# Neighbourhood attention with products by four heads; token sums between halves of units; channel transforms copied by VectorE

## The reference, cut to what matters

```
for l in range(2):                                   # first block
    h = rms_norm(x, g_mix[l]); proj = h @ w_in[l]
    y_a = mla_mixer(...); y_b = dilated_mixer(...)
    y_c = neighbourhood_mixer(...)                   # 8 heads of 64, softmax over a window, then @ v
    merged = sum(sigmoid(gate_i) * (y_i @ w_pi[l]))
    x = x + merged @ w_o[l]
    h = rms_norm(x, g_ffn[l])
    x = x + (silu(h @ w1[l]) * (h @ w3[l])) @ w2[l]
x = rms_norm(x, g_final)
for l in range(2):                                   # second block
    h = layer_norm(x) * (1 + scale) + shift
    q, k, v, ... = split(h @ w_in2[l])
    y_attn = attention(rope(rms(q)), rope(rms(k)), v) * silu(g_a)
    y_conv = cb * short_conv(cc * cu) * silu(g_c)
    y_four = real(fft2(fu)) @ f_mix * silu(g_f)
    x = layer_norm(ALPHA * x + (1 + gate) * (concat(y) @ w_out[l])) * g + b
```

## Time and profile before

| | us |
|---|---|
| median of 3 runs | 2564.07 (2562.38 to 2568.13) |
| the profiled execution: time | 2568.33 |
| its span in the profile | 2566.5 |
| TensorE busy, matmuls | 2493.5 (97%) |
| GpSimd busy | 1938.6 (76%) |
| VectorE, ScalarE busy | 1128.2 (44%), 669.2 (26%) |

### The profile page before, as it was taken

One profiled execution on the slowest core, in us unless ns is written; L12 is line 12 of the kernel. 1 busy time (PEld: TensorE's weight loads), 2 busy tenths in 40 slices (PEclk: granted clock), 3 DMA queues, 4 the chain that ended last, 5 costly groups with the idle time before them and its releaser, 6 DMA issues.

```text
span 2566.5 us, 38041 instructions
## 1 busy us (share of the span) xinstructions
PE 2493.5 (97%) x12990; PEld 2002.1 (78%) x12990; DVE 1128.2 (44%) x1592; ACT 669.2 (26%) x1320; POOL 1938.6 (76%) x1567
## 2 busy tenths in 40 slices
PE   7999999999999999999999999999999999999998
PEld 6776777777888887777787777888887877778776
DVE  6557453224312125557634224422225338550765
ACT  4445232112201013435314111210002215231351
POOL 7788656899989889878764889998988574448704
PEclk9999999999999999999999999999999999999998
DMA  4233321223333323333421223333333121112301
GB/s 146 88 107 116 132 66 62 90 92 92 98 98 98 93 92 96 95 94 120 145 82 36 88 90 98 98 98 91 97 98 95 60 88 58 42 35 90 99 1 66
DMA packets 67569, 226.62 MB, mean 88 GB/s; under 512 B 7552, under 2 KB 16256, under 8 KB 66944
## 3 DMA queue, kind: packets, MB, share of 16 engines
q1 hardware_dynamic: 66016, 221.32, 27.4%
q10 hardware_dynamic: 1440, 3.79, 0.4%
HBM read 222.99 MB, written 2.10 MB: 88 GB/s over the span
## 4 chain that ended last, share of the span: by engine, by line
POOL 36%; PE 32%; issue 20%; DVE 5%; DMA 4%; POOLq 2%; ACT 0%; SPq 0%; DVEq 0%; ACTq 0%
POOL whi L477 18%; POOL wlo L480 12%; PE ps L575 8%; PE ps L577 8%; PE ps L576 8%; POOL raw L496 3%; POOL ada_acc L498 3%; DMA raw<-w_gate 2%; DMA raw<-w_abc 1%; PE ps L718 1%; PE ps L685 1%; DVE q_parts L1930 1%; POOLq L479 1%; PE ps L629 1%; PE ps L1133 1%
## 5 line engine op out<-in xcount | busy, mean ns | idle before, releaser
L477 POOL TENSOR_TENSOR whi<-raw,one 128x512 fp32r<-128x512 f32 (+3 forms) x732 | 793.4, 1084 | 505.0 <-PE ps L577 413.5
L480 POOL TENSOR_TENSOR wlo<-raw,whi 128x512 fp32r<-128x512 f32 (+3 forms) x732 | 955.7, 1306 | 57.4
L575 PE MATMUL ps<-h,whi 128*128 128x512 f32 (+1 forms) x1952 | 778.2, 399 | 27.3 <-POOL wlo L480 17.2
L576 PE MATMUL ps<-h,whi 128*128 128x512 f32 (+1 forms) x1952 | 764.6, 392 | 0.0
L577 PE MATMUL ps<-h,wlo 128*128 128x512 f32 (+1 forms) x1952 | 764.4, 392 | 0.0
L575 PEld LDWEIGHTS ps<-h,whi 128*128 128x128 f32 (+1 forms) x1952 | 368.1, 189 | 122.4 <-POOL wlo L480 30.0
L577 PEld LDWEIGHTS ps<-h,wlo 128*128 128x128 f32 (+1 forms) x1952 | 367.8, 188 | 79.1
L576 PEld LDWEIGHTS ps<-h,whi 128*128 128x128 f32 (+1 forms) x1952 | 368.4, 189 | 77.3 <-issue 2.4
L575 PE MATMUL ps<-y,whi 128*128 128x512 f32 x640 | 251.1, 392 | 0.6 <-DVE y L1852 0.6
L576 PE MATMUL ps<-y,whi 128*128 128x512 f32 x640 | 249.2, 389 | 0.0
L577 PE MATMUL ps<-y,wlo 128*128 128x512 f32 x640 | 249.2, 389 | 0.0
(11 more groups left out here) (290 smaller groups left out, 3059.7 us busy)
## 6 DMA issues: line engine op xcount, KB each, us to landing
raw<-w SPq DMA_DIRECT2D x120, 512.0 KB, 3.5
raw<-w_abc SPq DMA_DIRECT2D x68, 512.0 KB, 3.5
raw<-w_ada SPq DMA_DIRECT2D x48, 512.0 KB, 3.5
raw<-w_gate SPq DMA_DIRECT2D x48, 512.0 KB, 3.6
raw<-w_in SPq DMA_DIRECT2D x44, 512.0 KB, 3.5
raw<-w_pac SPq DMA_DIRECT2D x16, 512.0 KB, 3.5
raw<-w_o SPq DMA_DIRECT2D x16, 512.0 KB, 3.5
raw<-w_out SPq DMA_DIRECT2D x16, 512.0 KB, 3.5
```

The costliest lines, as they stand in the source:

```text
L477: pool.tensor_tensor(whi[:, s, r], raw[:, s, r], one[:, 0:1].to_broadcast([P, cols // 2]), ALU.mult).then_inc(hi_made, 1)
L480: pool.tensor_tensor(wlo[:, s, r], raw[:, s, r], whi[:, s, r].bitcast(F32), ALU.subtract).then_inc(made, 1)
L575: nc.tensor.matmul(out, whi[:, s, w], moving[:, c, :], start=(c == 0), stop=False)
L576: nc.tensor.matmul(out, whi[:, s, w], rest[:, c, :], start=False, stop=False)
```

## The change

Seven edits:

1. Start of a layer: square sums at the half of unit 2, the spread of the factor at the half of unit 3, and the three latent sums at the halves of unit 4, unit 15 and the unit behind unit 16, instead of between units.
2. Neighbourhood attention with `group=4`, and four slots for turned tiles instead of three.
3. Feed-forward: the first two units write banks 2 and 3 and do not wait for a bank; square sums at the half of the second unit, spread at the half of the third. VectorE's first round of the loop is written out with those banks.
4. `residual_and_input`: the rests of chunks 6 and 7 come before the squares of chunks 6 and 7.
5. Second block: `two_units` writes banks 2 and 3.
6. Channel transforms copied by VectorE, after its first three maxima, instead of by ScalarE.
7. `put_y` of the convolution's two tiles moves from before the attention into its steps 4 and 8; the attention's output gets a tile of its own (`out_g`) instead of `ytmp`.

```
-        slots_c = [pt_flat[:, i * C_WIN:(i + 1) * C_WIN] for i in range(3)]
+        slots_c = [pt_flat[:, i * C_WIN:(i + 1) * C_WIN] for i in range(4)]
...
-            def unit(s, n, moving, rest, m=P, each=None, halfway=None):
-
-                pe.wait_ge(bank_free[s], free_n[s].next())
+            def unit(s, n, moving, rest, m=P, each=None, halfway=None, bank=None):
+
+                if bank is None:
+                    pe.wait_ge(bank_free[s], free_n[s].next())
                 split_n[s].next()
-                tiles(s, s, n, moving, rest, m, each=each, halfway=halfway).then_inc(unit_done[s], 1)
+                tiles(s if bank is None else bank, s, n, moving, rest, m, each=each, halfway=halfway).then_inc(unit_done[s], 1)
...
                 unit(0, DC, h_hi, h_lo, each=chunk_by_chunk(h_ready, h_n, DC))
-                unit(1, DC, h_hi, h_lo)
-                square_sums().then_inc(nsum_done, 1)
-                unit(0, DC, h_hi, h_lo)
-                spread_rs()
-                unit(1, DC, h_hi, h_lo)
+                unit(1, DC, h_hi, h_lo, halfway=lambda: square_sums().then_inc(nsum_done, 1))
+                unit(0, DC, h_hi, h_lo, halfway=spread_rs)
+                unit(1, DC, h_hi, h_lo, halfway=lambda: token_sums(sqa[0:1], last=False))
                 pairs(B_TILES - 1, DC, h_hi, h_lo)
-                unit(0, DC, h_hi, h_lo)
+                unit(0, DC, h_hi, h_lo, halfway=lambda: token_sums(sqa[1:2], first=False))
                 unit(1, DC, h_hi, h_lo, m=HD)
                 pe.wait_ge(rsb_ready, rb_n.next())
-                pe.wait_ge(bank_free[0], free_n[0].now() + 1)
-                token_sums(sqa[0:2])
-                token_sums(sqa[2:3], bank=7).then_inc(nsum_done, 1)
...
-                unit(0, DC, h_hi, h_lo)
+                unit(0, DC, h_hi, h_lo, halfway=lambda: token_sums(sqa[2:3], bank=7).then_inc(nsum_done, 1))
...
                 attention(C_HEADS, c_scores, c_value, 2, ring_c, slots_c, (2, 3, 4, 5), (7,), 1,
-                          between=c_qk_rest, ready=v_read)
+                          group=4, between=c_qk_rest, ready=v_read)
...
-                        unit(0, DC, h_hi, h_lo, each=chunk_by_chunk(h_ready, h_n, DC))
-                        square_sums().then_inc(nsum_done, 1)
-                        unit(1, DC, h_hi, h_lo, halfway=spread_rs)
+                        unit(0, DC, h_hi, h_lo, each=chunk_by_chunk(h_ready, h_n, DC), bank=2)
+                        unit(1, DC, h_hi, h_lo, halfway=lambda: square_sums().then_inc(nsum_done, 1), bank=3)
+                        unit(0, DC, h_hi, h_lo, halfway=spread_rs)
+                        unit(1, DC, h_hi, h_lo)
...
-                def channel_parts():
-                    for i in range(8):
-                        t, blk = i // 4, i % 4
-                        act.wait_ge(ch_done, ch_n.next())
-                        nc.scalar.activation(ac[:, blk, t].rearrange("p k c -> p (k c)"), ps[5 + 2 * (i % 2)][:, 0:2 * P],
-                                             ACT.Copy).then_inc(ch_used, 1)
...
-                        if m >= 1:
+                        if 1 <= m < DC - 1:
                             rest_and_square(m - 1, gain)
-                    rest_and_square(DC - 1, gain)
+                    for m in (DC - 2, DC - 1):
+                        rest(m, gain)
+                    for m in (DC - 2, DC - 1):
+                        square(m)
...
                 for t in range(2):
-                    put_y(t, conv_out[t])
                     free_n[t].next(15)
+
+                def channel_parts():
+                    for i in range(8):
+                        t, blk = i // 4, i % 4
+                        dve.wait_ge(ch_done, chd_n.next())
+                        nc.vector.tensor_copy(ac[:, blk, t].rearrange("p k c -> p (k c)"),
+                                              ps[5 + 2 * (i % 2)][:, 0:2 * P]).then_inc(ch_used, 1)
+
+                def conv_rest(i):
+                    if i in (4, 8):
+                        put_y(i // 4 - 1, conv_out[i // 4 - 1])
```

More of the change, by code:

```diff
@@ L596, in pairs, with two_units @@
                         unit(s, n, moving, rest)
-            def two_units(n, moving, rest, each):
+            def two_units(n, moving, rest, each, banks):
                 per = n // 2
                 for s in range(2):
-                    pe.wait_ge(bank_free[s], free_n[s].next())
                     split_n[s].next()
@@ L609, in two_units @@
                             pe.wait_ge((half_split, split)[c // per][s], split_n[s].now())
-                        nc.tensor.matmul(ps[s][:], whi[:, s, w], moving[:, c, :], start=(c == 0), stop=False)
-                        nc.tensor.matmul(ps[s][:], whi[:, s, w], rest[:, c, :], start=False, stop=False)
-                        last = nc.tensor.matmul(ps[s][:], wlo[:, s, w], moving[:, c, :], start=False, stop=(c == n - 1))
+                        nc.tensor.matmul(ps[banks[s]][:], whi[:, s, w], moving[:, c, :], start=(c == 0), stop=False)
+                        nc.tensor.matmul(ps[banks[s]][:], whi[:, s, w], rest[:, c, :], start=False, stop=False)
+                        last = nc.tensor.matmul(ps[banks[s]][:], wlo[:, s, w], moving[:, c, :], start=False, stop=(c == n - 1))
                         if c == per - 1:
@@ L1062, in _ @@
                     head_sums(t - 2)
+                    if 2 <= t < 4:
+                        free_n[t % 2].next()
                 unit(0, DC, h_hi, h_lo)
@@ L1340, in _ @@
                     ud_n[s].next(4)
[L1341 removed]
+                attention(C_HEADS, C_WIN, lambda i: ring_c[i % 4], True, y_block(Y_C, 4, c_order, [out_c]), ring_c, slots_c, 1, group=4)
                 sig = prob[:].rearrange("p a b -> p (a b)").rearrange("p (c t) -> p c t", t=T)
@@ L1538, in attention @@
             def attention(n_heads, cols, maximum, move_pt, y_out, ring, slots, o_banks, out, r_bank, gated=False, between=None,
-                          group=2, behind=0, later=None):
+                          group=2, behind=0, later=None, aside=None):
                 n = NQB * n_heads
@@ L1794, in _ @@
                 attention(C_HEADS, C_WIN, c_max, False, y_block(Y_C, 4, c_order, [out_c]), ring_c, slots_c, (7,), [out_c], 1,
-                          between=rest_of_queries_and_keys)
+                          group=4, between=rest_of_queries_and_keys)
                 free_n[0].next(6)
@@ new lines, in feed_forward @@
+                def feed_forward(j, banks):
+                    dve.wait_ge(unit_done[0], ud_n[0].next())
+                    nc.vector.tensor_tensor(tmp[1], ps[banks[0]][:], rsb[:], ALU.mult).then_inc(bank_free[0], 1)
+                    dve.wait_ge(unit_done[1], ud_n[1].next())
+                    nc.vector.tensor_tensor(tmp[2], ps[banks[1]][:], rsb[:], ALU.mult).then_inc(bank_free[1], 1)
+                    free_n[0].next()
+                    dve.wait_ge(mg_ready, mg_n.now())
+                    mg_n.next()
+                    dve.wait_ge(silu_ready, si_n.next())
+                    dve.wait_ge(bank_free[1], free_n[1].next())
+                    nc.vector.tensor_tensor(tmp[0], tmp[2], prob[:, 0, 0:T], ALU.mult).then_inc(ff_ready, 1)
+                    dve.wait_ge(mhi_ready, mhi_n.next())
+                    nc.vector.tensor_tensor(y[:, bass.ds(j + 8, 1), :].rearrange("p a t -> p (a t)"), tmp[0],
+                                            y[:, bass.ds(j, 1), :].rearrange("p a t -> p (a t)").bitcast(F32),
+                                            ALU.subtract).then_inc(mg_ready, 1)
@@ L1855, in _ @@
+                for part, n in enumerate(FF_PARTS):
+                    peeled = 1 if part == 0 else 0
+                    if peeled:
+                        feed_forward(0, (2, 3))
+                    with repeat(dve, n - peeled, [(ud_n[0], 1), (ud_n[1], 1), (free_n[0], 1), (free_n[1], 1), (si_n, 1),
+                                                  (mhi_n, 1), (mg_n, 1)]) as j:
+                        feed_forward(j + peeled, (0, 1))
                     if part < 2:
```

52 lines of the change are left out of this document (18 added, 34 removed).

## The result

The changed kernel takes 2569.55 us (median of 20 runs, 2567.58 to 2578.90), the kernel before 2564.54 (20 runs beside them, 2561.19 to 2571.82). The ratio is 1.0025, 95% interval [1.0017, 1.0032]: **slower by about 6 us** (5 by the medians), where 2.5 us faster was forecast. The profiled execution of after took 2568.98 us, 0.6 under its median; that of before 2568.33, 3.8 over the median of its 20.

What follows compares the result with a forecast made beforehand. TensorE, busy for 97% of the span, was taken to bound the kernel. The terms -5.8 - 1.2 - 5.6 - 2.9 + 2.1 + 4.1 + 6.8 = -2.5 us, off the median 2564.1, gave 2561.6 us, range 2553 to 2568.

Steps and rivals of the forecast that it cites:

- the base: Terms were made against the profiled execution, 4.3 us above the runs' median, but taken off that median, 2564.1 us.
- the start of layer 1: Square sums asked for before their squares are ready push out half a unit, 2.72, and the spread waits 1.35: +4.1 us.
- the token sums of the latents: Three groups of eight keep the clock up, gaining 1.76 a layer less 0.3 for holds: -2.9 us over two layers.
- rival C: Slower: the clock falls in new gaps at layer starts and in the attention, about 9.5 us more, 2571; chance 0.13.
- Layer 2: Start of layer 2: the spread, wanted half a unit earlier, waits 2.0 us for the roots: +2.1 us.
- Attention: Neighbourhood attention by four heads: waits for ScalarE's copy at block ends outweigh the switches saved, +6.8 us over two layers.
- the switches saved: In the attention, fewer switches to the products and back: about 0.3 us each four heads, 2.4 a layer.
- Feed-forward: Start of a feed-forward: both waits go and the clock stays up, 2.9 us a layer, -5.8 us.
- channel transforms: Third product comes 2.3 us earlier in each layer, 1.3 more from full clock in the second, +0.3 elsewhere: -5.6 us.
- banks: Banks 2 and 3 in the second block remove the wait for the query tile's copy and square: -1.2 us.
- A: Rival: in the attention ScalarE keeps up and the saved switches count, -4.8 instead of +6.8 us, 2550; chance 0.13.
- B: Rival: the starts of the layers do not wait because the roots are early, 6.2 us less, 2555; chance 0.12.

Runs made afterwards that it cites:

- e1: Changed kernel with the square sums and spread of a layer's start back between whole units, as in the kernel before: 2561.01 us, ratio 0.9974 to before.
- e6: Changed kernel with the last eight latent token sums ahead of the last unit instead of at its half: 2568.47 us, ratio 1.0014 to before.
- e9: Changed kernel, groups of four kept, with the high part of the attention's block output made by GpSimd instead of ScalarE: 2570.06 us, ratio 1.0020 to before.
- e4: Changed kernel with layer starts, attention by four heads and spread latent sums all undone: 2553.58 us, ratio 0.9950 to before.
- e2: Changed kernel with the neighbourhood attention back at groups of two heads and three slots: 2566.10 us, ratio 1.0004 to before.
- e3: Changed kernel with the 24 token sums of the latents back in one piece: 2571.45 us, ratio 1.0020 to before.
- e7: Changed kernel with a layer start's square sums at the half of unit 3 and the spread behind unit 3: 2557.62 us, ratio 0.9972 to before.
- e5: Changed kernel, groups of four kept, with the attention's block output two heads later on ScalarE and VectorE: 2573.20 us, ratio 1.0028 to before.
- e11: Changed kernel with the old order of the last residuals, squares of chunk 6 ahead of the rest of chunk 7: 2571.68 us, ratio 1.0026 to before.

## Why the prediction was wrong, step by step

Measured is 8.0 us over the forecast of 2561.6. The parts, read in the traces, make 5.2 of it (+2.7 instead of -2.5), the base from which they were counted 4.3, and the profiled execution of after, 0.6 under its own median, 0.6; the end of the program, where before ran at the lower clock, takes 2.1 off. Three steps failed: the start of layer 1, the token sums of the latents, and the base. The first two share one cause, VectorE's small steps held by GpSimd; the larger term of the first, 2.5 us of lower clock, stood at nothing in the sum.

- **"Start of a layer", layer 1: +4.1, measured +8.0.** The pushed half unit (2.72) was right. The wait at the spread was put at 1.35 and is 2.7, and the clock term stood in rival C alone, at 0.13: it fell for 8.4 us of work instead of 3.4. The 1.5 us allowed from the root to the end of the roots was the length of the chain with few holds; the two held steps made it 2.6 (37.77 to 40.34). The earlier trace rows had 2.4 for the same chain (1013.6 to 1016.05); the forecast took 0.9 off for fewer holds, and no row shows them fewer. The step before it (unit 2 done at 34.3) took the lower clock to last as long as before, 3.4 us; behind a gap of 4.2 us it lasted over 5.0 us of work, and it fell again for 3.4 us behind the gap ahead of the spread. e1 shows the part's whole price.
- **Layer 2: +2.1, measured +2.6.** Mechanism and size right.
- **"Token sums of the latents": -2.9, measured -0.3.** The clock term (1.76) was right. Of the wait, "I take 0.3 off", 1.36 came, and three groups cost 0.2 more than one. The text had named the very thing, GpSimd holding an instruction on a chain with 2.72 us of cover. It priced the hold as if it fell seldom; on a chain of ten small steps beside a GpSimd that cuts weights, two are held, 0.8 to 1.1 us each. That GpSimd holds them is read from their ends, which fall together with its own; no run takes GpSimd away from the chain. e6 shows that the short cover is what makes it cost: with a whole unit of cover one step is still held and the 1.36 go.
- **Attention: +6.8, measured +6.7**, and by its items: block ends 4.0 (4.2 forecast; 3 x 1.33), first group 0.9 (1.0), reciprocals 0.8 (1.0), and as the remainder 2.0 for the switches saved (2.4; the forecast's own 0.25 each four heads makes 2.0, it had rounded up to 0.3). The mechanism was right as well: the forecast has VectorE done at T + 2.4, and ScalarE's chain end at T + 4.6; in after T is 387.70, VectorE's multiplication ends at T + 2.4, and the products start at T + 4.5. What it did not see is that a second chain ends only 0.4 us earlier (e9), so that its reading, the output's 1.10 us ahead of copy 11, does not say what is won by taking the output away.
- **Feed-forward: -5.8, measured -6.5; channel transforms: -5.6, measured -5.8; banks: -1.2, measured -1.5.** Right, with the clock terms (1.7 at each feed-forward, 1.3 at the second channel transform) as worked out.
- **The base.** The 4.3 us between before's profiled execution and its median were taken off as if after would have them too. It does not: the two profiled executions differ by 0.65 us, the medians by 5.0. The granted clock tells where this comes from. Among the executions of before that were timed beside e1 to e4, the 13 with a mean clock of 0.991 have a median of 2564.3 us, the 5 with 0.989 one of 2568.5, and the profiled execution has 0.989. So it had more time at 1.2 GHz than is usual for its kernel. As an estimate: a mean clock lower by 0.002 is 10 us more of the 2566 at half the clock, and half of that is lost, 5 us. Of these, 2.1 us lie in TensorE's last 5 us. The profiled execution of after has 0.993, as 12 of its 20 have. An offset of that kind belongs to one execution and not to the kernel.

Corrected by the table: +10.6 - 0.3 + 6.7 - 6.5 - 0.8 - 5.8 - 1.5 = +2.4, and small differences of both signs elsewhere make the 2.7 of the table's end. The forecast was -2.5; the 4.9 between are 4.4 from the layer starts and 2.6 from the latents, less 0.7 from the feed-forwards, 0.8 that was not counted, and 0.6 from banks, channel transforms and attention.

Of the rivals, A (attention gains) and B (no wait at the starts) were refuted by e2 and e1. C named the right place, the clock behind the gap of 4.4 us in layer 1, and there it fell. In the attention, with gaps of 1.1 us, it stays up in after; but of the 18 attentions by four heads in these traces two have a stretch at 1.2 GHz (layer 2 in e3, layer 1 in e7, 1.6 and 1.5 us), and of the 10 by two heads none. So C's place in the attention is possible but seldom.

## What to carry to other kernels

An operation moved between two halves of a unit halves the cover of the chain that it starts, so the chain has to be priced with its holds in, not at its shortest length: here, with GpSimd cutting weights, two VectorE steps of 0.17 us took about 1 us each in both chains. Half a unit can still be enough where the rest of the chain is done before (e7). Moving a request earlier gives nothing where the data's time is set elsewhere; moving it later (e7) removed both the wait and the fall of the clock behind it. A forecast made against one profiled execution should look at that execution's granted clock first. When a change has several parts, count along the unchanged instructions of both traces: that gives each part's price in one look, and the best kernel here is the change with half of its parts turned round.

## What the runs showed that was not expected

The held steps come in any order of the sums: even e6 has a step of 0.99 us; the only question is what covers it. In e5 a piece of work of 1.1 us moved by two heads did not shorten the block but made it 0.6 us longer (11.1 instead of 10.54), because the last exponentials of the next group came late, behind VectorE's rest of that output. And every changed version, whatever its start, has 0.4 to 0.9 us less idle time ahead of layer 2; neither the order of the residuals (e11) nor any of the three parts undone in e4 is the cause, and it stays open.
